# Own-result waits taken out of the mixing stages of a two-block transformer kernel

## The chip, the core and the metric

The kernel runs on one core of one Trainium2 chip. The metric is the device time of one execution in microseconds. Three executions of the kernel before took 4094.2, 4097.06 and 4097.98 us, so the median is 4097.06 us.

## What is computed

The input is 512 tokens of 1024 values. The reference runs two layers of a first block (which is computed in `block1`) and then two layers of a second one (`block2`), all in float32. Cut to what matters here:

```python
# block 1, one layer
h = h + 0.5 * _swiglu_ffn(_rms_norm(h, ffn1_norm[i]), ffn1_w_gate_up[i], ffn1_w_down[i])
u = _rms_norm(h, mix_norm[i])
q, k, v, ca, cg = jnp.split(u @ w_in[i], SPLITS, axis=-1)
attn = _sliding_window_attention(q, k, v, sinks[i])       # 8 heads, window 128, after partial rope
conv = _conformer_conv(ca, cg, ...)                       # 31 taps, layer norm, silu
mixed = jnp.concatenate([_rms_norm(attn, ...), _rms_norm(conv, ...)], axis=-1)
h = h + mixed @ w_out[i]
h = h + 0.5 * _swiglu_ffn(_rms_norm(h, ffn2_norm[i]), ...)
h = h + jax.nn.sigmoid(h @ w_ple_gate[i]) * _rms_norm(p[i] @ w_ple[i], ple_norm[i])
...
# block 2, one layer: the same frame, with three mixers side by side
#   gated delta rule (6 heads, short convolutions, chunks, a running state),
#   sparse attention with a compressed branch (6 heads),
#   stick-breaking attention (4 heads)
# then an FFN with a convolution of 3 taps and the gated per-layer embedding
return _rms_norm(h, final_norm)
```

## The kernel before, in words

Activations lie transposed in SBUF: 128 partitions times 8 chunks of 512 tokens. A weight matrix is streamed from HBM in units of 128 x 1024 values. TensorE (PE) multiplies in a format that drops the low bits of float32, so every weight unit and every activation tile is split in two: ScalarE (ACT) writes the high part (`act_split`, L381), VectorE (DVE) the rest (`dve_split`, L385), and `pe_unit` (L399 to L401) does three matmuls for each chunk. The result of a unit lies in one of two PSUM banks, and VectorE takes it out ("evicts" it).

There is no scheduler. Every engine runs a list of instructions written out by hand, and the engines meet on semaphores: an instruction ends with `.then_inc(s["name"], 1)`, and `wait_ge(s["name"], n)` stands ahead of whichever needs it. In the feed-forward stages ScalarE and VectorE wait for results of their own only where the next operation reads or overwrites them. In the other stages (the "mixing stages") nearly every operation of these two engines is followed at once by a wait for its own semaphore, whatever comes next; `st.up(name)` counts up how far that semaphore is.

The mixing stages of a layer of block 1 are the input projection (14 units), the attention with its convolution, normalisations and per-layer embedding, and the output projection (8 units). The attention runs over 16 pairs of heads and blocks: PE `scores` (L821), VectorE `scale` (L1203, which adds the mask and takes the maximum), ScalarE `exps` (L1003), PE `turn` (L833), VectorE `turn_back` (L1215), PE `values`. Between them stand taps of the convolution on all four engines (L854 PE, L1144 VectorE, L935 ScalarE, L734 GpSimd), the layer norm (L1285 to L1300), and the per-layer embedding, one tile for each pair: PE L807, VectorE L1189, ScalarE L987. At the end come the tiles of the attention output (L1242, PE L860) and their parts (L1312, L1249).

In block 2 the input projection (22 units, evicted by `evict`, L2823 and L2829, with `post` for the rotated tiles, L2791 to L2798) is interleaved with the sparse attention (L2080, L2240, L2149, L2250); then follows the delta rule with its triangular inverse (PE L1748, L1756, L1764; VectorE L1786; ScalarE L1773, L1779) beside the stick-breaking attention (PE L1903, VectorE L1960, ScalarE L1931, L1936), then the running state, the normalised heads (`dve_lo`, `dve_gate`, `act_hi`: L2332, L2308, L2316, L2320; PE L2292), and the embedding (PE L2349, VectorE L2911). After the last layer, VectorE scales the eight chunks of `h` (L2958), and each is stored as it is done.

ScalarE evaluates functions from tables. Where the next function needs another table, an ACT_TABLE_LOAD stands ahead of the ACTIVATE that needs it. An instruction carries one wait; where there are more, the rest are put on what stands ahead of it, the table load or a wait alone in the engine's queue.

## Time and profile before

| | |
|---|---|
| median of three executions | 4097.06 us |
| the profiled execution | 4096.91 us |
| its span, from the first to the last instruction | 4095.1 us |
| granted TensorE clock, mean over the span | 0.965 |
| instructions of VectorE, ScalarE and GpSimd with busy time | 3149, 2242 and 366 |
| VectorE and ScalarE busy | 57% and 39% of the span |

The page of the profile divides the span into busy time by engine. A stage is read by asking for the same sums in a stretch of the span. A timeline lists the instructions of a stretch in order of time; two of one engine whose start and length are both known show whether the second began before the first had ended. The clock is a share of 2.4 GHz: 1.00 is that level, 0.50 is 1.2 GHz.

### The profile page before, as it was taken

To read this page: it belongs to the slowest core of one execution; us is meant where nothing else is said; L and a number is where in the kernel's file an instruction comes from. 1 tells how busy PE (TensorE), PEld (TensorE's weight loads), DVE (VectorE), ACT (ScalarE), POOL (GpSimd) and SP (SyncE) were. 2 spreads that over 40 slices of the span, in tenths; PEclk is the share of its full clock that TensorE was granted. 3 is DMA by queue.
4 is the path that set the end of the run, shared out by engine and by line. 5 is a ranking of instruction groups with operands and counts; after the bars stand their busy time and mean duration, and the time that the engine had idled before them with its cause. 6 is when DMAs were issued, how large, how long until landed. Compare 5 with 4: busy or idle time off the path is not lost. (4 is left out here: it accounts for less than half of the span.)

```text
span 4095.1 us, 47766 instructions
## 1 busy us (share of the span) xinstructions
PE 3912.0 (96%) x17866; PEld 3105.5 (76%) x17866; DVE 2340.5 (57%) x3149; ACT 1583.4 (39%) x2242; POOL 491.2 (12%) x366
## 2 busy tenths in 40 slices
PE   8999989999999997999989989899999999989997
PEld 6888658888788865888867667788877667778886
DVE  5455756445544575645567643675576763376656
ACT  3224643223322464322343534343343444433333
POOL 1001711000000172000020012200010002210002
PEclk9999979999999997999999989899999998999999
DMA  4333103333333320333331100122333100022222
GB/s 148 96 98 110 55 16 98 98 97 108 88 98 97 110 66 13 95 98 98 105 103 62 42 6 1 47 93 98 98 105 100 55 31 1 6 71 94 98 98 77
DMA packets 87028, 315.08 MB, mean 77 GB/s; under 512 B 10016, under 2 KB 10400, under 8 KB 86176
## 3 DMA queue, kind: packets, MB, share of 16 engines
q1 hardware_dynamic: 83664, 302.43, 23.7%
q10 hardware_dynamic: 3152, 9.74, 0.7%
q8 instruction: 143, 2.34, 0.2%
q14 instruction: 69, 0.57, 0.0%
HBM read 307.94 MB, written 2.10 MB: 76 GB/s over the span
## 5 line engine op out<-in xcount | busy, mean ns | idle before, releaser
L381 ACT ACTIVATE wh<-raw 128x1024 fp32r<-128x1024 f32 x564 | 597.8, 1060 | 1613.0 <-PE ps L401 1305.5
L399 PE MATMUL ps<-xh,wh 128*128 128x512 f32 x2336 | 918.3, 393 | 16.8 <-DVE xl L464 10.0
L400 PE MATMUL ps<-xl,wh 128*128 128x512 f32 x2336 | 911.3, 390 | 0.0
L401 PE MATMUL ps<-xh,wl 128*128 128x512 f32 x2336 | 911.1, 390 | 0.0
L385 DVE TENSOR_TENSOR wl<-raw,wh 128x1024 fp32r<-128x1024 f32 x564 | 693.8, 1230 | 201.8 <-ACT wh L381 197.8
L399 PEld LDWEIGHTS ps<-xh,wh 128*128 128x128 f32 x2336 | 440.1, 188 | 113.0 <-issue 20.0
L400 PEld LDWEIGHTS ps<-xl,wh 128*128 128x128 f32 x2336 | 440.1, 188 | 94.3 <-issue 3.6
L401 PEld LDWEIGHTS ps<-xh,wl 128*128 128x128 f32 x2336 | 440.0, 188 | 91.9
L399 PE MATMUL ps<-fh,wh 128*128 128x512 f32 x1016 | 397.3, 391 | 4.4 <-DVE wl L385 4.4
L400 PE MATMUL ps<-fl,wh 128*128 128x512 f32 x1016 | 395.4, 389 | 0.0
L401 PE MATMUL ps<-fh,wl 128*128 128x512 f32 x1016 | 395.3, 389 | 0.0
L443 POOL TENSOR_TENSOR rstd<-rstd,sq 128x512 f32<-128x512 f32 x77 | 116.4, 1512 | 1693.7 <-ACT sq L438 1692.7
L555 DVE SCALAR_TENSOR_TENSOR h<-ps,h 128x512 f32<-128x512 f32 x144 | 99.5, 691 | 317.5 <-PE ps L401 245.4
L399 PEld LDWEIGHTS ps<-fh,wh 128*128 128x128 f32 x1016 | 190.7, 188 | 48.2 <-DVE wl L385 8.3
L401 PEld LDWEIGHTS ps<-fh,wl 128*128 128x128 f32 x1016 | 190.7, 188 | 39.8
L400 PEld LDWEIGHTS ps<-fl,wh 128*128 128x128 f32 x1016 | 190.7, 188 | 39.6 <-issue 0.5
L409 PE MATMUL ps<-xh,wh 128*128 128x512 f32 x448 | 196.6, 439 | 18.6 <-PEq L1363 9.8
L625 DVE TENSOR_TENSOR ubuf<-ps,rstd 128x512 f32<-128x512 f32 x88 | 60.9, 692 | 264.7 <-PE ps L401 264.7
L734 POOL TENSOR_TENSOR y<-y,tap_out 128x512 f32<-128x512 f32 x120 | 173.7, 1448 | 76.7 <-ACT tap_out L935 69.2
L411 PE MATMUL ps<-xh,wl 128*128 128x512 f32 x448 | 178.2, 398 | 0.0
L410 PE MATMUL ps<-xl,wh 128*128 128x512 f32 x448 | 177.7, 397 | 0.0
L621 DVE TENSOR_TENSOR gbuf<-ps,rstd 128x512 f32<-128x512 f32 x88 | 60.9, 692 | 197.8 <-PE ps L401 197.7
(463 smaller groups left out, 5694.7 us busy)
## 6 DMA issues: line engine op xcount, KB each, us to landing
raw<-in_w SPq DMA_DIRECT2D x564, 512.0 KB, 3.5
con<-in_consts SPq DMA_DIRECT2D x1, 2052.5 KB, 14.1
h<-in_x SPq DMA_DIRECT2D x4, 512.0 KB, 7.2
p_t<-in_p ACTq DMA_DIRECT2D x4, 512.0 KB, 3.7
w1k<-in_w1c ACTq DMA_DIRECT2D x2, 1024.0 KB, 4.8
w1v<-in_w1c ACTq DMA_DIRECT2D x2, 1024.0 KB, 7.2
out<-h SPq DMA_DIRECT2D x8, 256.0 KB, 2.1
dup_k<-roped ACTq DMA_DIRECT2D x8, 128.0 KB, 2.8
```

What stands on the lines that cost most here:

```text
L381: nc.scalar.activation(wh[k % 2][:, :], raw[k % 4][:, :], ACT.Copy).then_inc(s["w_hi"], 1)
L385: nc.vector.tensor_tensor(wl[k % 2][:, :], raw[k % 4][:, :], wh[k % 2][:, :].bitcast(F32), ALU.subtract).then_inc(s["w_lo"], 1)
L399: nc.tensor.matmul(DB[k % 2][:, :], a, hi(q), start=(q == order[0]), stop=False)
L400: nc.tensor.matmul(DB[k % 2][:, :], a, lo(q), start=False, stop=False)
L401: last = nc.tensor.matmul(DB[k % 2][:, :], b, hi(q), start=False, stop=(q == order[-1]))
L409: nc.tensor.matmul(DB[k % 2][:, :], a, hi(q), start=start and n == 0, stop=False)
L410: nc.tensor.matmul(DB[k % 2][:, :], a, lo(q), start=False, stop=False)
L411: last = nc.tensor.matmul(DB[k % 2][:, :], b, hi(q), start=False, stop=stop and n == len(chunks) - 1)
L443: nc.gpsimd.tensor_tensor(acc[:, :], acc[:, :], sq[:, n % 2, :], ALU.add).then_inc(s["sq_add"], 1)
L555: nc.vector.scalar_tensor_tensor(h[:, j, :], DB[k % 2][:, :], factor, h[:, j, :], ALU.mult, ALU.add).then_inc(s["bank"], 1)
L621: v.tensor_tensor(gbuf[:, :], DB[k % 2][:, :], rstd[:, :], ALU.mult).then_inc(s["bank"], 1)
L734: nc.gpsimd.tensor_tensor(y[:, ct, :], y[:, ct, :], tap_out[:, i % 3, :], ALU.add)\
```

## The change

On VectorE, ScalarE and GpSimd, the wait for an operation's own semaphore is taken out after nearly every operation of the mixing stages. It stays where the very next operation reads or overwrites the result, and a wait is put in front of later operations that do so (the diff takes out 137 lines with a wait and puts in 25). Increments, instructions and buffers stay as they are. In the built program 1062 instructions of VectorE, 846 of ScalarE and 100 of GpSimd have lost a wait, and 86 of VectorE and 72 of ScalarE name one that they did not name before, partly because a wait has moved from one instruction to its neighbour.

The core of the diff; the same edit is made in some hundred places:

```diff
@@ scale and exps of the attention, block 1
                                     v.tensor_tensor_reduce(sm[:, m % 2, e, 0:w], ...)\
                                         .then_inc(s["max_ready"], 1)
-                                    dve.wait_ge(s["max_ready"], st.up("max_ready"))
...
                                       bias=negm[:, n:n + 1], accum_out=den[:, n:n + 1]).then_inc(s["prob"], 1)
-                                    act.wait_ge(s["prob"], st.up("prob"))
@@ layer norm
                                     for q in range(CT):
                                         v.tensor_tensor(y[:, q, :], y[:, q, :], rstd[:, :], ALU.mult)\
                                             .then_inc(s["ln_ready"], 1)
-                                        dve.wait_ge(s["ln_ready"], st.up("ln_ready"))
@@ a wait that is kept, further down
                             def sink_in(b):
+                                dve.wait_ge(s["max_ready"], (b + 1) * H1)
                                 v.tensor_tensor(es[:, b, 0, :], negm[:, b * H1:(b + 1) * H1], g("sinks"), ALU.add)\
                                     .then_inc(s["sink_in"], 1)
-                                dve.wait_ge(s["sink_in"], st.up("sink_in"))
@@ rotate, block 1
+                                dve.wait_ge(s["bank"], o + U1_IN + (9 if n == 0 else n + 10))
                                 v.tensor_tensor(fbuf[:, :], buf[:, :], cos[:, :], ALU.mult).then_inc(s["dve_step"], 1)
+                                dve.wait_ge(s["rot_mm"], n + 1)
                                 dve.wait_ge(s["dve_step"], st.up("dve_step"))
-                                dve.wait_ge(s["rot_mm"], n + 1)
@@ output projection
                                 v.tensor_tensor(h[:, n, :], DB[u % 2][:, :], h[:, n, :], ALU.add)\
                                     .then_inc(s["bank"], 1)
-                                dve.wait_ge(s["bank"], st.up("bank"))
                                 if n < DC - 1:
                                     dve_split(dve, s, st, 0, u + 2)
+                                dve.wait_ge(s["bank"], u + 1)
                                 dve_tile(dve, s, st, n, g("ffn2"), made + 8 + n)
@@ evict, block 2
                                 if kind in ("rope", "tok"):
-                                    dst = (gbuf, ubuf)[posted.index(n) % 2][:, :]
+                                    p_ = posted.index(n)
+                                    dst = (gbuf, ubuf)[p_ % 2][:, :]
+                                    if due(p_ - 1):
+                                        dve.wait_ge(s["post_done"], p_ - 1)
...
                                     v.tensor_tensor(dst, src, rstd[:, :], ALU.mult).then_inc(s["bank"], 1)
-                                    dve.wait_ge(s["bank"], st.up("bank"))
@@ the last scaling
                                     v.scalar_tensor_tensor(h[:, j, :], h[:, j, :], gfin[:, 8 + j:9 + j], rstd[:, :],
                                                            ALU.mult, ALU.mult).then_inc(s["fin_h"], 1)
-                                    dve.wait_ge(s["fin_h"], st.up("fin_h"))
```

No instruction changes its place on any engine. What changes is what each waits for. On VectorE, in the attention of block 1 (pair 9, then the reciprocal of the layer norm), before and then after; `ISA sm` is `scale`, `ISA negm` the read of its maximum, and line numbers differ between the two texts:

```order
L1203 ISA sm,negm<-ps,con,negsink 128x256 [waits prob,s_mm,pt_ready]
L1203 ISA negm 128x1
L1203 ISA sm,negm<-ps,con,negsink 128x256 [waits max_ready]
L1203 ISA negm 128x1
L1189 COPY e_t<-ps 128x512 [waits ple_mm,max_ready]
L1215 COPY pt<-ps 128x512 [waits pv_mm,pt_mm,ple_ev]
L1221 TENSOR_TENSOR es<-negm,small_73 128x8 [waits pt_ready]
L1290 RECIPROCAL rstd<-rstd 128x512 [waits ln_root,sink_in]
L1293 TENSOR_TENSOR y<-y,rstd 128x512 [waits dve_step]
```

```order
L1181 ISA sm,negm<-ps,con,negsink 128x256 [waits prob,s_mm]
L1181 ISA negm 128x1
L1181 ISA sm,negm<-ps,con,negsink 128x256
L1181 ISA negm 128x1
L1168 COPY e_t<-ps 128x512 [waits ple_mm]
L1192 COPY pt<-ps 128x512 [waits pv_mm,pt_mm]
L1198 TENSOR_TENSOR es<-negm,small_73 128x8 [waits max_ready]
L1260 RECIPROCAL rstd<-rstd 128x512 [waits ln_root]
L1263 TENSOR_TENSOR y<-y,rstd 128x512 [waits dve_step]
```

Every row but the last has lost the wait for the row ahead of it; the last reads what the reciprocal writes and keeps it. On ScalarE, at the root of the layer norm's variance (L1025), before and then after:

```order
L992 ACTIVATE gbuf,ss<-o_tok 128x512 [waits o_ready,prob]
L1025 ACT_TABLE_LOAD [waits var_mm]
L1025 ACTIVATE rstd<-ps,con 128x512 [waits o_sum]
L987 ACTIVATE tap_out<-e_t 128x512 [waits ple_ev,ln_root]
L1003 ACT_TABLE_LOAD [waits max_ready,pt_mm]
```

```order
L981 ACTIVATE gbuf,ss<-o_tok 128x512 [waits o_ready]
L1011 ACT_TABLE_LOAD
L1011 ACTIVATE rstd<-ps,con 128x512 [waits var_mm]
L977 ACTIVATE tap_out<-e_t 128x512 [waits ple_ev]
L991 ACT_TABLE_LOAD [waits max_ready]
```

The ACTIVATE had two waits, and the one for PE's result (`var_mm`) stood on the table load; now it stands on the ACTIVATE, and the load waits for nothing.

## Rows read from the trace of the kernel before

**Rows 1.** The page: TensorE's busy time over the span, its share, instructions.

```profile
PE 3912.0 (96%) x17866; PEld 3105.5 (76%) x17866; DVE 2340.5 (57%) x3149; ACT 1583.4 (39%) x2242; POOL 491.2 (12%) x366
```

**Rows 2.** Busy time by stretch: length, then engines, granted clock, DMA, GB/s.

```profile
716.80:819.20 102.40, 102.40 (x453) 84.79 (x452) 41.91 (x49) 25.44 (x29) 0.00 (x0) 1.00 0.33 98
463.00:606.00 143.00, 116.91 (x424) 75.57 (x424) 81.95 (x156) 70.74 (x139) 56.01 (x44) 0.81 0.04 12
2106.00:2361.00 255.00, 249.98 (x1191) 180.08 (x1189) 185.04 (x339) 109.89 (x180) 9.95 (x7) 0.99 0.20 65
2361.00:2403.00 42.00, 35.54 (x146) 24.48 (x145) 23.39 (x37) 7.84 (x13) 5.34 (x5) 0.67 0.03 13
2403.00:2579.00 176.00, 167.18 (x1134) 138.80 (x1132) 65.14 (x118) 80.10 (x120) 41.40 (x38) 0.97 0.01 4
2579.00:2635.00 56.00, 45.68 (x191) 35.04 (x191) 32.78 (x50) 18.60 (x28) 9.03 (x7) 0.79 0.08 25
2375.40:2406.10 30.70, 27.15 (x85) 17.78 (x86) 11.12 (x22) 7.92 (x11) 5.74 (x6) 0.50 0.00 1
```

**Rows 3.** Waits of TensorE over the span: total us, times, longest.

```profile
PE ps L807 <- DVE e_t L1189: 18.7, 10, 4.9
PE ps L2349 <- DVE e_t L2911: 12.7, 4, 4.7
PE ps L860 <- DVE o_tok L1242: 12.5, 2, 6.2
```

**Rows 4.** Timeline of VectorE, feed-forward stage: start, length, instruction.

```profile
709.47 0.69 DVE L625 TENSOR_TENSOR ubuf<-ps,rstd 128x512 f32<-128x512 f32 x1 [3.06 <-PE ps L401]
710.20 0.69 DVE L628 TENSOR_TENSOR fbuf<-ubuf,sbuf 128x512 f32<-128x512 f32 x1
710.81 1.22 DVE L385 TENSOR_TENSOR wl<-raw,wh 128x1024 fp32r<-128x1024 f32 x1
```

**Rows 5.** Timeline of ScalarE, feed-forward stage, then attention.

```profile
704.09 1.06 ACT L381 ACTIVATE wh<-raw 128x1024 fp32r<-128x1024 f32 x1 [3.41 <-PE ps L401]
705.06 0.61 ACT L613 ACTIVATE sbuf<-gbuf 128x512 f32<-128x512 f32 x1
...
472.81 2.98 ACT L935 ACTIVATE tap_out<-upad,small 128x512 f32<-128x512 f32 x4
476.37 0.72 ACT L935 ACTIVATE tap_out<-upad,small 128x512 f32<-128x512 f32 x1 [0.58 <-POOL y L734]
```

**Rows 6.** Timeline, attention of block 1, layer 0, VectorE and then TensorE.

```profile
540.11 3.35 DVE L1290 RECIPROCAL rstd<-rstd 128x512 f32<-128x512 f32 x1
...
543.50 2.87 DVE L1293 TENSOR_TENSOR y<-y,rstd 128x512 f32<-128x512 f32 x4
546.40 0.48 DVE L1203 CUSTOM_DVE_ANT_0 sm<-ps,con,negsink 128x256 f32<-128x256 f32 x1
...
546.93 0.48 DVE L1203 CUSTOM_DVE_ANT_0 sm<-ps,con,negsink 128x256 f32<-128x256 f32 x1
...
547.46 0.69 DVE L1189 COPY e_t<-ps 128x512 f32<-128x512 f32 x1
...
548.30 0.77 PE L807 MATMUL ps<-p_hi,wh 128*128 128x512 f32 x1 [4.94 <-DVE e_t L1189]
```

**Rows 7.** Timeline of block 2's last mixing stage, layer 1.

```profile
3600.86 0.75 DVE L2308 SCALAR_TENSOR_TENSOR dec<-ps,small,z_t 128x512 f32<-128x512 f32 x1
...
3605.40 0.80 PE L2349 MATMUL ps<-p_hi,wh 128*128 128x512 f32 x1 [4.66 <-DVE e_t L2911]
```

**Rows 8.** Timeline, the last scaling.

```profile
4085.52 6.26 DVE L2958 SCALAR_TENSOR_TENSOR h<-h,gfin,rstd 128x512 f32<-128x512 f32 x8
```

**Rows 9.** Timeline of ScalarE, a table load in the attention.

```profile
531.64 1.28 ACT L1025 ACT_TABLE_LOAD   x1 [4.11 <-PE ps L889]
...
532.94 0.69 ACT L1025 ACTIVATE rstd<-ps,con 128x512 f32<-128x512 f32 x1
```

**Rows 10.** Timeline of VectorE beside GpSimd, end of the input projection.

```profile
463.75 1.48 DVE L1126 TENSOR_TENSOR fbuf<-ubuf,cos 128x512 f32<-128x512 f32 x1
```

More of the change, by code:

```diff
@@ L556, in dve_ffn @@
                                                    ALU.mult, ALU.add).then_inc(s["bank"], 1)
-                    evicted = st.up("bank")
                     if j < DC - 1:
@@ L560, in dve_ffn @@
                     if g == len(GROUPS) - 1 and gain is not None:
-                        dve.wait_ge(s["bank"], evicted)
+                        dve.wait_ge(s["bank"], k + 1)
                         dve_tile(dve, s, st, j, gain, x_n + j, hi, lo)
@@ L621, in dve_swiglu @@
             v.tensor_tensor(gbuf[:, :], DB[k % 2][:, :], rstd[:, :], ALU.mult).then_inc(s["bank"], 1)
-            st.up("bank")
             dve_split(dve, s, st, i, k + 2)
@@ L1158, in _ @@
                                     out = (v_t, ubuf)[n % 2]
+                                    if due(n // 2) and n % 2:
+                                        dve.wait_ge(s["conv_in"], n // 2)
                                 elif n == 9:
@@ L1460, in read @@
                             .then_inc(s["bank"], 1)
-                        st.up("bank")
                     def later_taps(half):
@@ L1579, in dve_rows @@
                         .then_inc(s["dve_step"], 1)
[L1580 removed]
+                    st.up("dve_step")
                     v.memset(ones, 1.0).then_inc(s["dve_step"], 1)
@@ L2790, in post @@
                                 if kind == "rope":
+                                    dve.wait_ge(s["bank"], o + posted[p_] + 1)
+                                    if due(p_):
+                                        dve.wait_ge(s["post_done"], p_)
                                     v.tensor_tensor(sbuf[:, :], buf[:, :], cos[:, :], ALU.mult)\
                                         .then_inc(s["dve_step"], 1)
+                                    dve.wait_ge(s["post_mm"], p_ + 1)
                                     dve.wait_ge(s["dve_step"], st.up("dve_step"))
-                                    dve.wait_ge(s["post_mm"], p_ + 1)
                                     v.tensor_tensor(buf[:, :], BK[p_ % 2][:, :], sin[:, :], ALU.mult)\
@@ L2799, in post @@
                                         .then_inc(s["post_done"], 1)
-                                    dve.wait_ge(s["post_done"], st.up("post_done"))
                                 else:
@@ L2805, in post @@
                                         .then_inc(s["post_done"], 1)
-                                    dve.wait_ge(s["post_done"], st.up("post_done"))
                             def evict(n):
@@ L2919, in _ @@
                                     .then_inc(s["bank"], 1)
-                                dve.wait_ge(s["bank"], st.up("bank"))
                                 if n < DC - 1:
@@ L2926, in _ @@
                                     dve.wait_ge(s["dve_step"], st.up("dve_step"))
+                                dve.wait_ge(s["bank"], u + 1)
                                 dve_tile(dve, s, st, n, g("ffn"), made + n)
@@ L2940, in _ @@
                                     .then_inc(s["bank"], 1)
-                                dve.wait_ge(s["bank"], st.up("bank"))
                                 if n < DC - 2 or n == DC - 2 and after:
```

154 lines of the change are left out of this document (29 added, 125 removed).

## The prediction, made before the changed kernel was run

> **What bounds the kernel now.** I read the page first. TensorE is busy for 3912.0 of 4095.1 us [rows 1]. So 183.1 us of the span are open to a change that does nothing to the matmuls, and the first question is where they lie. The sums by stretch answer it. In a stretch of the feed-forward stage TensorE has no idle time at all, 102.40 of 102.40 us, at full clock. In the attention of block 1 it idles 143.00 - 116.91 = 26.1 us; in block 2's input projection with the sparse attention 255.00 - 249.98 = 5.0 us; in the start of the delta rule 42.00 - 35.54 = 6.5 us; in its main part 176.00 - 167.18 = 8.8 us; and from the running state to the output projection 56.00 - 45.68 = 10.3 us [rows 2]. That is 56.7 us for one layer of each block, some 113 us for both. The rest lies at the start, at the joints of the blocks and after the last matmul. The diff touches nearly only these mixing stages, so this is the place to look.
>
> The second question is who ends TensorE's idle time. The waits say: mostly VectorE. L807 waits 18.7 us for the copy L1189, L860 waits 12.5 us for L1242, and L2349 waits 12.7 us for L2911 [rows 3]. The timeline in front of the longest wait of L807 shows VectorE with no pause: a reciprocal, four multiplications, two `scale`, the copy, each right behind the other, and then TensorE starts after 4.94 us of idleness [rows 6]. That is the kind of place where time between two VectorE instructions becomes time of the kernel.
>
> **What one wait costs.** The feed-forward stage has both kinds of neighbours. L628 reads what L625 writes and waits for it: the starts lie 710.20 - 709.47 = 0.73 us apart, which is L625's 0.69 and 0.03 to 0.04 of gap. L385 behind it has no wait for L628, and starts 710.81 - 710.20 = 0.61 us after it, 0.08 before it has ended [rows 4]. So a wait for an own result costs VectorE 0.73 - 0.61 = 0.12 us when the next instruction is otherwise ready. ScalarE: behind L381 (1.06 us) the Silu without such a wait starts after 705.06 - 704.09 = 0.97 us, 0.09 early. In the attention four L935, which wait each for the one ahead, take 2.98 us; with 0.72 for one, the starts lie (2.98 - 0.72) / 3 = 0.75 apart, 0.03 late [rows 5]. Again 0.12 us. I take 0.12 for both engines.
>
> The Trainium skill speaks against this. "VectorE: DVE Perf Modes", section "The DRAIN you can't avoid", says that eight copies take the same time with a semaphore after each as with one at the end, and its rules advise to count operations and not semaphores; by that the sum below would be 0. The same section sends the reader on to two instructions with no wait between them, where the later one starts early unless it is held, and with that the 0.08 us of [rows 4] agrees. The page's comparison counts increments and not waits, so I give the first reading a chance but not the first place.
>
> **The parts of the change.** Waits go at 1062 instructions of VectorE and 846 of ScalarE. All of them at 0.12 us would be 229 us, more than there is idle time, so the number of waits says nothing; only those in a row of work that TensorE waits for count. I went through the timeline of each mixing stage and counted, in the stretches that end with an idle TensorE, the instructions that start 0.03 to 0.04 us behind their neighbour because of a wait that goes.
>
> - *Attention of block 1.* Ahead of the first scores: 3. Ahead of the long wait of L807: 9 (the four L1293 and two L1203 of [rows 6] with the copies around them). In the next two pairs, through ScalarE's Silu tiles too: 8. At 573 to 575 us: 2. From the reciprocal L1297 to L860: 6. From there to the output projection some 10 stand in a row, but TensorE idles only 0.6 us there, so I count 5. Together 33, times 0.12 is 4.0 us a layer, 8.0 us for two.
> - *Running state to output projection, block 2.* About 10 in the rows that end at L2349 and L2292, as L2308 and its neighbours [rows 7]: 1.2 us, 2.4 for two layers.
> - *Main part of the delta rule.* About 9, mostly the pairs of L1786 and the three L1960: 1.1 us, 2.2 for two layers.
> - *Block 2's input projection and the start of the delta rule.* TensorE idles 11.5 us in them; waits for row operations and norms, where I find few neighbours: 8, so 1.0 us, 2.0 for two layers.
> - *The last scaling.* Eight in a row take 6.26 us and nothing covers them [rows 8]. Seven waits go: 7 x 0.12 = 0.8 us. This is the surest term.
> - *Input and output projections of block 1, the embedding gate.* TensorE is busy there, VectorE waits for it. The work of `pe_unit` hides the edits, and I count 0. They would be worth something only if VectorE were late for a bank.
> - *Table loads.* A load takes 1.28 us. At L1025 it starts after ScalarE has idled 4.11 us for TensorE, and the root follows at 532.94 [rows 9]. In the new program the load waits for nothing and lies inside those 4.11 us, so the root starts 1.28 us earlier. The same is so at a dozen loads, but few of them lead to TensorE. I take 1 us for each layer's attention and 0.3 for the compressed scores of each layer of block 2: 2.6 us.
> - *Waits that are added* (`post_done` at evictions, `bank` at `rotate`, `z_ready` at the squares). Each is for an instruction that stands several places earlier on the same engine. Nothing queues behind them that would not have queued before. From 0 to 0.12 us each, and nearly none on the path; I take 0.
> - *GpSimd's 100 waits.* It is busy 56.01 us in the attention and its sums are ready before they are asked for: 0.
>
> The sum is 8.0 + 2.4 + 2.2 + 2.0 + 0.8 + 2.6 = 18.0 us. The profiled execution took 4096.91 us, 0.15 less than the median, and 4096.91 - 18.0 = 4078.9. I predict **4079 us**.
>
> The bounds. Below, if the waits cost nothing where they stand, it is 0. Above, I count every own wait in the long rows of VectorE that touch an idle TensorE at all, also where TensorE is idle only for a part of them: 75 in an attention stage, about 20 in each of three stages of block 2. That is 2 x (75 + 60) = 270, with the 7 at the end 277, times 0.12 = 33 us, and with the loads 36 us: 4061 us. I stay near the lower of the two counts, since in the other the same idle time is used twice. Also, a pair of the attention goes TensorE, VectorE, ScalarE, TensorE; when one leg is shorter the next is often not ready.
>
> **Rivals.**
>
> *Nothing.* The waits of one engine for another take over: VectorE reaches its next instruction 0.12 us earlier and waits there for TensorE. For it: in the attention VectorE is busy for only 81.95 of 143.00 us, so for much of it it waits for someone. Against it: in front of L807 and L860 it does not. The time would be that of before less the last scaling and the surest loads, 4092 to 4097 us.
>
> *The clock gives back more.* TensorE runs at 0.50 of its clock for all of 2375.4 to 2406.1 us, with 27.15 us of work in it [rows 2]; at full clock that work would take 13.6 us. What went before it is a stretch in which TensorE paused for VectorE. If shorter pauses keep it from falling there in both layers, 2 x 13 = 26 us come on top of a part of the sum: 4055 to 4068 us. For it: the change makes exactly these pauses shorter. Against: they get shorter by a tenth, and the clock falls in the same places in both layers although these differ by some us.
>
> *Slower, by the clock.* The same mechanism the other way. The mixing stages have 0.81, 0.67 and 0.79 of the clock [rows 2]. If TensorE's work comes in tighter bursts between the same long waits, the low level could last longer. At half clock a us of matmuls costs half a us. To undo 18 us and lose 8 more, the low level would have to last 52 us longer, where now a layer's attention has 143 x (1 - 0.81) x 2 = 54 us of it. It decides from 36 us of more low level on, below which the change still gains; the time would be near 4105 us. Nothing in the trace points that way, but one stretch of 30.7 us moved or doubled is a large part of it.
>
> *Slower, by the shared memory.* L1126 takes 1.48 us while GpSimd works beside it [rows 10], and a like operation 0.69 [rows 6]. If VectorE's instructions shift so that more of them meet GpSimd's, each costs 0.8 us. GpSimd's own work stays the same, so what VectorE meets stays about the same in sum; ten more meetings on the path would be needed to take away 8 us. I put it with the rival above.
>
> **How the numbers follow.** A measurement of this kernel cannot tell less than 0.2%, 8.2 us, from no change. My forecast, 8 to 28 us faster: 0.58. More, through the clock: 0.14. Nothing: 0.19. Slower than by 8.2 us: 0.09. That makes faster 0.72, same 0.19, slower 0.09. The range reaches from the clock rival's middle to the middle of the rival in which nothing comes of it: 4057 to 4093 us, which leaves out about 0.05 below and 0.15 above.
>
> **What would show it.** In the profile after, four L1293 should take 2.87 - 3 x 0.12 = 2.5 us and eight L2958 6.26 - 0.8 = 5.4 us; if not, the price is wrong. The longest wait of L807 should fall from 4.9 to about 4, and that of L860 from 6.2 to about 5.5; if these stay while the rows on VectorE are shorter, another wait has taken their place. TensorE's idle time in an attention stage should be near 22 us. The feed-forward stretches should stay as they are. The table load of L1025 should lie before the end of TensorE's L889. The forecast is wrong if the mean clock over the span moves from 0.965 by more than 0.003, which is 12 us of the low level's difference, or if the rows are shorter and TensorE's idle time is not.

## The result, and the profile after

The changed kernel took 4056.95 us (median of four executions, 4049.91 to 4058.68), beside 4095.63 us (4088.59 to 4097.98) for the kernel before on the same chip: a ratio of 0.9904, with a 95% interval of 0.9892 to 0.9917. That is 38.7 us, where 18 were forecast. The direction and the places were right, the size was off by a factor of two, and the time lies just below the range. The profiled execution took 4058.68 us, with a span of 4056.9, against 4096.91 and 4095.1 before.

The page after answers to [rows 1]:

```profile
PE 3895.8 (96%) x17866; PEld 3094.0 (76%) x17866; DVE 2287.4 (56%) x3149; ACT 1543.7 (38%) x2242; POOL 491.6 (12%) x366
```

Here is already a part of the answer. The span has fallen by 38.2 us. TensorE's idle time is 4056.9 - 3895.8 = 161.1, before it was 183.1, so it has fallen by 22.0. The other 16.2 us are TensorE's *busy* time: the same 17866 matmuls took less time. My sum was one of idle time only. (These are two single executions, and the division isn't one by cause, as the executions at equal clock show further down.)

Sums by stretch of the kernel after (length, then PE, PEld, DVE, ACT and POOL busy with their instructions, granted clock, DMA share, GB/s): the attentions of layers 0 and 1 of block 1, block 2's first input projection, the half-clock stretch at the start of its delta rule, and a stretch of the feed-forward stage:

```profile
462.70:595.30 132.60, 110.12 (x425) 71.18 (x424) 75.59 (x157) 65.52 (x139) 55.94 (x44) 0.86 0.04 12
1487.80:1619.30 131.50, 110.36 (x426) 70.73 (x425) 75.04 (x157) 65.66 (x139) 56.09 (x44) 0.86 0.04 13
2062.30:2335.10 272.80, 260.83 (x1232) 188.53 (x1233) 185.07 (x346) 116.60 (x191) 14.99 (x11) 0.98 0.20 66
2348.50:2379.20 30.70, 28.14 (x88) 18.48 (x88) 10.36 (x22) 9.23 (x13) 5.73 (x6) 0.50 0.00 1
703.80:806.20 102.40, 102.40 (x453) 84.81 (x452) 42.40 (x48) 26.45 (x30) 0.00 (x0) 1.00 0.32 96
```

Beside [rows 2]: the feed-forward stretch is untouched, the 30.7 us at half clock are still there in full, and layer 0's attention has gone from 143.0 to 132.6 us at a clock of 0.86 instead of 0.81. Two of the same sums of the kernel before that were not shown, layer 1's attention and the first input projection:

```profile
1500.40:1640.40 140.00, 113.65 (x424) 74.13 (x424) 81.30 (x156) 70.75 (x139) 56.03 (x44) 0.83 0.04 12
2083.80:2362.10 278.30, 264.18 (x1237) 190.51 (x1237) 195.49 (x346) 120.06 (x191) 15.33 (x11) 0.97 0.20 65
```

TensorE's waits over the span after, which answer to [rows 3] (total us, times, longest; L802 was L807, L855 was L860, L2268 was L2349):

```profile
PE ps L802 <- DVE e_t L1168: 13.1, 11, 3.8
PE ps L855 <- DVE o_tok L1217: 12.3, 2, 6.2
PE ps L2268 <- DVE e_t L2818: 11.9, 4, 4.3
```

And the timeline of the kernel after where [rows 6, 8, 9] stood before (start, length, instruction, idle time before it and what ended it):

```profile
524.72 1.28 ACT L1011 ACT_TABLE_LOAD   x1
525.81 0.59 PE L884 MATMUL ps<-ubuf,con 128*128 128x512 f32 x1
526.24 1.02 PE L884 MATMUL ps<-fbuf,con 128*128 128x512 f32 x2
527.30 0.69 ACT L1011 ACTIVATE rstd<-ps,con 128x512 f32<-128x512 f32 x1 [1.29 <-PE ps L884]
...
534.76 3.35 DVE L1260 RECIPROCAL rstd<-rstd 128x512 f32<-128x512 f32 x1
...
538.14 2.50 DVE L1263 TENSOR_TENSOR y<-y,rstd 128x512 f32<-128x512 f32 x4
540.56 0.48 DVE L1181 CUSTOM_DVE_ANT_0 sm<-ps,con,negsink 128x256 f32<-128x256 f32 x1
...
540.96 0.48 DVE L1181 CUSTOM_DVE_ANT_0 sm<-ps,con,negsink 128x256 f32<-128x256 f32 x1
...
541.37 0.69 DVE L1168 COPY e_t<-ps 128x512 f32<-128x512 f32 x1
...
542.20 0.76 PE L802 MATMUL ps<-p_hi,wh 128*128 128x512 f32 x1 [3.80 <-DVE e_t L1168]
...
4047.99 5.39 DVE L2862 SCALAR_TENSOR_TENSOR h<-h,gfin,rstd 128x512 f32<-128x512 f32 x8
```

The price on VectorE was right nearly to the digit: four multiplications take 2.50 us (2.87 before, 2.5 forecast), eight scalings 5.39 (6.26 before, 5.4 forecast), and from the first of these multiplications to TensorE's start it is 4.06 us instead of 4.80. On ScalarE three of the convolution's L929 (L935 before) now stand in a row of 1.93 us, so their starts lie (1.93 - 0.72) / 2 = 0.60 us apart, where it was 0.75. The table load has moved as forecast, ahead of the end of L884.

To see all of it I cut every trace at the same VectorE instructions. Length, in brackets TensorE's idle time, and behind it the time at a granted clock of 0.50, all in us of one execution:

| stage | before | after | expected gain | length's gain | of it idle time |
|---|---|---|---|---|---|
| attention, layer 0 | 143.1 (26.1) 54.6 | 132.6 (22.5) 37.5 | 5.0 | 10.5 | 3.6 |
| attention, layer 1 | 140.0 (26.3) 47.8 | 131.5 (21.1) 37.5 | 5.0 | 8.5 | 5.2 |
| block 2, first projection and start of delta rule | 317.5 (20.4) 43.0 | 310.6 (16.5) 34.5 | 1.3 | 6.9 | 3.9 |
| the same, layer 1 | 307.4 (14.6) 36.7 | 303.3 (11.9) 32.6 | 1.3 | 4.1 | 2.7 |
| main part, both layers | 358.7 (18.8) 22.7 | 357.5 (14.0) 35.2 | 2.2 | 1.2 | 4.8 |
| running state to output, both | 107.9 (22.8) 41.0 | 104.6 (23.0) 34.2 | 2.4 | 3.3 | -0.2 |
| tail | 22.0 (19.9) 19.9 | 21.1 (19.0) 18.8 | 0.8 | 0.9 | 0.9 |
| the rest (feed-forward, block 1's projections, joints, start) | 2698.5 (34.2) 17.0 | 2695.7 (33.1) 13.7 | 0 | 2.8 | 1.1 |

### The profile page after: what moved, and what is told of

It is laid out like the page before. It is cut to its first block and busy times, and to the rows that moved or that the text cites. A ratio compares the mean times of both kernels' runs of the same rounds, so it can differ in the third digit from the quotient of the medians.

```text
span 4056.9 us, 46747 instructions
## 1 busy us (share of the span) xinstructions
PE 3895.8 (96%) x17866; PEld 3094.0 (76%) x17866; DVE 2287.4 (56%) x3149; ACT 1543.7 (38%) x2242; POOL 491.6 (12%) x366
## 3 DMA queue, kind: packets, MB, share of 16 engines
q1 hardware_dynamic: 83664, 302.43, 23.8%
## 5 line engine op out<-in xcount | busy, mean ns | idle before, releaser
L385 DVE TENSOR_TENSOR wl<-raw,wh 128x1024 fp32r<-128x1024 f32 x564 | 694.4, 1231 | 191.7 <-ACT wh L381 190.7
L399 PEld LDWEIGHTS ps<-xh,wh 128*128 128x128 f32 x2336 | 440.0, 188 | 112.6 <-issue 19.9
```

The costliest lines, as they stand in the source:

```text
L385: nc.vector.tensor_tensor(wl[k % 2][:, :], raw[k % 4][:, :], wh[k % 2][:, :].bitcast(F32), ALU.subtract).then_inc(s["w_lo"], 1)
L399: nc.tensor.matmul(DB[k % 2][:, :], a, hi(q), start=(q == order[0]), stop=False)
```

## The experiments

Each was timed beside the kernel before on the same chip. A ratio is to that one. Times of both kernels scatter by up to 12 us between executions, so I read a stage from the trace, and the sum from the ratio. A trace is one execution, and its clock scatters too.

**Executions at equal clock.** Every execution lists its mean granted clock, and the time goes with it. Of 75 executions of the kernel before, timed beside the experiments, the 16 at 0.965 took 4098.95 us on average, and the six at 0.970 took 4089.29 us (4088.69 to 4089.70). The changed kernel's five at 0.970 took 4057.65 us (4055.61 to 4058.68). At the same mean clock the change is worth 31.6 us, then, and only some 7 of the 38.7 us come with the higher clock, although TensorE's busy time differs by 16.2 us in the two traces. (An equal mean doesn't say that the clock is low in the same places.)

**One engine at a time.** The same diff, its lines for VectorE alone (`e1_vector_only`), and for ScalarE alone (`e2_scalar_only`):

```diff
-                                    dve.wait_ge(s["max_ready"], st.up("max_ready"))     # e1, and so on
...
-                                    act.wait_ge(s["prob"], st.up("prob"))               # e2, and so on
```

> Only VectorE's part of the change; ScalarE and GpSimd wait for their own results as before. Own waits theory (most of the gain lies in VectorE's rows ahead of TensorE's waits, L807 and L860 above all): 25 to 32 us faster than before, TensorE idle some 15 us less and busy some 12 us less. Rival, ScalarE's early table loads and its own waits carry half or more: under 18 us faster.

> Only ScalarE's part of the change, early table loads with it; VectorE and GpSimd as before. Own waits of VectorE as the main cause: 4 to 10 us faster. Rival, ScalarE carries half or more: 18 us faster or more. If the parts add up, this and the kernel with VectorE's part alone give 38 us together; if the two engines stand in one another's way, each alone gives less than its share.

VectorE alone: 4072.11 us (4068.34 to 4072.65), 0.9944 [0.9928, 0.9961], or 21.4 us. ScalarE alone: 4089.91 us (ten executions, 4083.41 to 4097.5), 0.9990 [0.998, 1.0], or 3.6 us, less than can be told from no change. Both are below what I had expected, 25 to 32 and 4 to 10 us. VectorE carries most of it, but together they make 25 us of 38.7. In the traces TensorE's idle time falls by 17.5 and 4.1 us, together 21.6 of the 22.0: idle time adds up. What doesn't is the rest, TensorE's busy time. In the attention stages the kernel with VectorE's part has the idle time of the changed one (21.8 and 21.9 us, against 22.5 and 21.1), but 44.4 us of half clock in each instead of 37.5, and takes 134.6 and 134.8 us. GpSimd's 100 waits are in neither kernel, and no run takes them out alone. That they are worth nothing is not shown; the idle times leave 0.4 us for them.

**The early table loads undone.** In the changed kernel, a wait for something long past is put ahead of ScalarE operations that follow a load. With it the wait that matters stands on the load again (of 102 loads 60 had a wait before, 32 after, 56 here):

```diff
+                                    act.wait_ge(s["stat_read"], 1)
                                     act.wait_ge(s["var_mm"], 1)
```

> The changed kernel with one long-satisfied wait in front of some 24 of ScalarE's operations that need another table, so that the wait for the other engine stands on the table load again, as before the change. The prediction's term (2.6 us for early loads): 2 to 5 us slower than the changed kernel. Rival, the early loads carry the excess over the forecast: 10 to 20 us slower than the changed kernel, so 18 to 28 us faster than before.

It took 4057.38 us, 0.9908 [0.9891, 0.9924], which can't be told from the changed kernel's 0.9904. Its attentions take 132.5 and 131.5 us, as in the changed kernel, and block 2's input projections 274.3 and 266.7 us instead of 272.8 and 266.4. The load of the layer norm's root starts behind TensorE again, timeline of ScalarE in this kernel:

```profile
526.87 1.28 ACT L1012 ACT_TABLE_LOAD   x1 [2.63 <-PE ps L884]
528.17 0.69 ACT L1012 ACTIVATE rstd<-ps,con 128x512 f32<-128x512 f32 x1
```

The root is late by nearly a us and nobody minds: its reader, the reciprocal L1260, starts only at 534.76 us in the rows above, when VectorE has come to it. Of my 2.6 us for the loads the 2 for the attentions were 0. For the other 0.6 the trace leaves room in the first projection, where half clock differs too (13.7 and 10.2 us); it isn't resolved.

**TensorE kept busy.** If busy time has fallen because the clock was low for less time, then matmuls that nobody needs, put into TensorE's pauses, should do a part of the same to the kernel before. The first version repeats matmuls that are there (`rotate(4)` four times more, `values` of pairs 10, 11 and 15 three, one and four times, the last embedding tile once):

```diff
-                                for e in range(2):
+                                for e in (0, 1) * FILL_VALUES.get(m, 1):      # {10: 4, 11: 2, 15: 5}
```

> The kernel before with all its waits; TensorE repeats matmuls that it does anyway, with the same inputs into the same bank, in five places of each attention stage of block 1 just ahead of its long idle times (four more of the last rotation, 3 and 1 more passes of the values of pairs 10 and 11, one more of the last embedding tile, 4 more of the values of pair 15). VectorE's and ScalarE's work is unchanged. Clock theory (shorter idle times keep TensorE's clock up, and that gave the other half of the gain): 8 to 16 us faster than before, with less time at clock 0.50 in 463 to 606 us. Rival, the clock's lower share in the low level was only a by-product: no change or up to 6 us slower.

4090.38 us (ten executions, 4088.8 to 4092.95), 0.9991 [0.9982, 1.0001]. Half clock fell to 30.7 and 27.3 us in the two attentions, and they got shorter by 3.3 and 1.7 us although TensorE has more to do. The kernel as a whole is 3.1 us faster than the 4093.48 us beside it, which can't be told from no change; I had expected 8 to 16.

The second puts more of them in, 9 ahead of the first scores, 12 ahead of L860 and some in three embedding tiles, in the kernel before and in the changed one:

```diff
+                            def filler(times):
+                                for _ in range(times):
+                                    mm(BK[4][:, :], c("ident"), cos[:, :], start=True, stop=True)
...
+                            filler(9)
                             scores(0)
```

> The kernel before with all its waits; TensorE fills its five long idle times in each attention stage of block 1 with 128x512 matmuls whose results nothing reads (9 ahead of the first scores, 12 ahead of L860) and with repeats of the embedding tiles 3, 4 and 7 (3, 1 and 2 more passes). The fills before were short matmuls of 64 columns and left a stretch of 20.5 us at clock 0.50. Clock theory: this stretch goes or shrinks too, the low level takes under 20 us of an attention stage (now some 50), each stage is 5 to 9 us shorter and the kernel 8 to 16 us faster than before. Rival, the low level costs nothing where TensorE waits anyway: low level shorter, time as before within 3 us.

> The changed kernel with the same fills. Clock theory: 5 to 12 us faster than the changed kernel, 42 to 50 us faster than before. Rival (the change has taken already what the clock can give): the same as the changed kernel within 3 us, or slower by the fills.

Before with it: 4094.13 us (4089.3 to 4097.29), 0.9997 [0.9988, 1.0006]. After with it: 4064.29 us (4056.98 to 4065.46), 0.9921 [0.9908, 0.9935]. Neither came near what the clock theory had asked for, 8 to 16 us and 42 to 50; the changed kernel without the fill took 4058.14 us in the same batch. From the one kernel with the fill to the other it is 29.8 us, at a median clock of 0.977 in both. Layer 1's attention is the clean pair, first the kernel before with the fill, then the changed one with it:

```profile
1499.20:1636.80 137.60, 126.23 (x503) 78.56 (x503) 81.99 (x158) 70.80 (x139) 56.13 (x44) 0.99 0.04 12
```

```profile
1485.30:1616.90 131.60, 126.01 (x503) 78.50 (x502) 75.76 (x156) 65.40 (x139) 55.99 (x44) 0.99 0.04 13
```

At a clock of 0.99 in both, TensorE's busy time is the same and the stage differs by 6.0 us (5.8 where it is cut at the same instructions): this is what the waits alone are worth where the clock plays no part. My count of 33 and 0.12 said 4.0. (Layer 0's pair, 142.9 and 131.6 us, isn't clean: its clocks are 0.93 and 0.99.) And without a wait taken out, the clock and the fill make 140.0 into 137.6. The changed kernel gains nothing by the fill (131.6 against 131.5), although it has 34 us less of half clock. The fill puts 15.7 us more of matmuls into the stage, so what it costs and what the clock gives back can't be told apart here. That low clock costs little where TensorE waits for the others anyway fits this, and isn't shown by it.

**Waits that I hadn't counted, put back.** In the changed kernel, 33 of VectorE's own waits for an attention stage return at pairs 0 to 8, at two embedding tiles and in the layer norm:

```diff
                                         .then_inc(s["max_ready"], 1)
+                                    if m <= 8:
+                                        dve.wait_ge(s["max_ready"], 2 * m + e + 1)
```

> The changed kernel with VectorE's own waits put back at 33 places of each attention stage that I had not counted, since TensorE is not idle behind them: the maxima and copies of pairs 0 to 8, two embedding tiles and the subtraction of the mean. The prediction's count: at most 2 us slower than the changed kernel. Rival, VectorE's row is what bounds the stage and every wait in it counts: 33 x 0.12 x 2 = 8 us slower.

> The changed kernel once more, beside the others on one chip: 35 to 40 us faster than before.

4062.66 us (4061.76 to 4066.98), 0.9924 [0.991, 0.9937], beside the changed kernel again in the same batch: 4058.14 us (4051.39 to 4061.90), 0.9909 [0.9895, 0.9923]. That is 4.5 us, between the 2 at most of my count and the rival's 8, with intervals that overlap. In the traces the stages are longer by 3.0 and 3.6 us (134.7 and 135.2 against 131.7 and 131.6). In layer 0 the waits themselves make up only 0.6 us of it: that is how much later VectorE has come, from the start of the stage, by 548 us. TensorE's idle time is 21.8 and 20.9 us against 21.2 and 21.1. The rest shows itself in two timelines of TensorE over the same pairs, first this kernel, then the changed one:

```profile
545.37 2.07 PE L816 MATMUL ps<-k_t,q_t 64*128 64x256 f32 x4
...
554.37 2.07 PE L816 MATMUL ps<-k_t,q_t 64*128 64x256 f32 x4
...
564.69 1.13 PE L816 MATMUL ps<-k_t,q_t 64*128 64x256 f32 x4
```

```profile
545.64 2.07 PE L816 MATMUL ps<-k_t,q_t 64*128 64x256 f32 x4
...
554.65 1.31 PE L816 MATMUL ps<-k_t,q_t 64*128 64x256 f32 x4
...
562.59 1.13 PE L816 MATMUL ps<-k_t,q_t 64*128 64x256 f32 x4
```

Up to 554 us the two run side by side. Then four scores take 2.07 us in the one and 1.31 in the other, and the next ones come 10.32 instead of 7.94 us later. The clock rows say why: the half-clock stretch begins at 540.2 and lasts 20.5 us here, and 13.7 us, from 541.4, there:

```profile
540.20:560.70 20.50, 16.73 (x49) 12.46 (x50) 9.50 (x24) 12.10 (x25) 8.81 (x7) 0.50 0.09 27
```

```profile
541.40:555.10 13.70, 10.86 (x29) 7.80 (x30) 6.48 (x16) 10.17 (x19) 7.51 (x6) 0.50 0.14 40
```

So 6.8 us more of half clock cost 2.4 us at this place. Was it the waits that set it off, or chance? The same stretch is 20.5 us long in layer 1 of this kernel too. In five traces with all of block 1's change and no fill it is, over both layers, 13.7 us seven times and 17.0 three times (once in two pieces), and never 20.5. So it was the waits; which of them is not known.

**One block at a time.** The diff's lines up to the end of `block1` only (with a few helpers that both blocks share), and those of `block2` only.

> The change in the code of block 1 (and the few lines shared by both), block 2 as before. My theory now: the attention stages give some 11 and 8.5 us as in the whole change, block 2 nothing, so about 20 us, 4075 us on a before of 4095; half clock in the two attention stages near 37.5 us each. By the first forecast (5.0 us for a stage) it would be 10 to 11 us. If the blocks help each other (a stage of block 2 that gains only because block 1 ended otherwise) it would be more or less than 20 by over 3 us.

> Block 2 changed, block 1 as before: the counterpart of the run with block 1 alone, which gave 23.8 us. If the blocks add, this one gives the rest, 38.3 less 23.8 or some 15 us: 4080 us on 4095.5, with the stages of block 2 as long as in the whole change (272.9, 37.8, 179.5, 52.4 and 266.4, 37.0, 178.0, 52.4) and the attentions at 143.1 and 140.0. If the gain of a block needs the other, it is off by over 3 us.

Block 1 alone: 4071.39 us (4069.86 to 4073.56), 0.9941 [0.9928, 0.9954], 23.8 us. Block 2 alone: 4080.63 us (4077.99 to 4084.76), 0.9965 [0.9951, 0.9978], 14.3 us. Sum 38.1, where the whole gave 38.7: within the noise the blocks add. The expectation was 3.8 us short for block 1 and held for block 2. For both the prediction was too low: 10 and 8 us. With block 1 the median clock rises from 0.966 to 0.971, with block 2 it stays at 0.966. In the trace of block 2 alone its stages, from its first projection on and with the tail, are 14.0 us shorter, 11.5 of them idle time, and half clock takes 162.7 us in them instead of 163.3. So block 2's gain came without a higher clock: here it was the waits that I had put too low.

**The clock held at full level.** 41 fillers for a stage, better placed and without repeats of real work: ahead of the first scores, ahead of two embedding tiles into the bank of the statistics, ahead of the last `turn` and of L860:

```diff
+                                if m == 11:
+                                    pe.wait_ge(s["ln_root"], 1)
+                                if m in (11, 12):
+                                    filler({11: 10, 12: 4}[m], STAT)
                                 if PLE_AT <= m < PLE_AT + DC:
```

> The kernel before with 41 matmuls of 128x512 more in each attention stage, of the identity and into banks that nobody reads then, put where TensorE idles longest (ahead of the first scores, ahead of two embedding tiles in mid stage, ahead of the last turn, ahead of L860). No wait of the change is gone. Clock theory: half clock falls from 54.6 and 47.8 us a stage to under 20, the stages shorten by 3 to 4 and by 2 to 3 us, to about 139.5 and 137.5, all of it 5 to 7 us of the kernel. If the whole gain of the change comes from waits alone, nothing: both stages stay at 143 and 140 although the clock is up.

> The same 41 matmuls a stage in the changed kernel. Clock theory: it has already got what the clock gives on the path, so the stages stay at 131.5 to 132.5 us and the time within 3 us of the changed kernel, 4057. Against the kernel with the same matmuls and the old waits the stages differ by the waits alone: 5.8 us as in the pair of dense kernels, 7 at most. If low clock still costs in the changed kernel, it gains 3 us or more and is the best version.

Before: 4090.69 us, 0.9986 [0.9978, 0.9995]. After: 4064.03 us, 0.9927 [0.9914, 0.994]. One of the first kernel's twelve executions took 5807.67 us, at a mean granted clock of 0.632; why the clock was low is not known, and the median doesn't depend on it. From the one to the other it is 26.7 us, at a median clock of 0.980 and 0.979. Layer 0's attention, before and then after, both with the fill:

```profile
461.60:601.40 139.80, 133.41 (x507) 78.28 (x507) 81.93 (x157) 70.72 (x139) 56.05 (x44) 1.00 0.04 12
```

```profile
461.00:596.40 135.40, 133.26 (x507) 78.23 (x506) 75.87 (x157) 65.36 (x139) 56.11 (x44) 1.00 0.04 12
```

At full clock the waits are worth 4.4 us here, and 6.1 in layer 1 (141.4 and 135.3). The clock theory was only half right: of the kernel before layer 0's stage is shorter by 3.3 us, but layer 1's is 1.4 longer than in the trace shown above. The changed kernel loses 2.8 to 3.8 us a stage by the fill, and there TensorE idles for only 2.1 us: what I put into pauses may have become the bound. No version with a fill beats the changed kernel; this one was expected within 3 us of 4057.

**The input projection of block 2.** The prediction had 1.0 us a layer for its waits and those of the delta rule's start behind it, and 0.3 for loads; "nothing", as the first expectation below has it, was my count for block 1's projections. First the waits are put back into the changed kernel, for VectorE (and at one place for ScalarE):

```diff
                                     v.tensor_tensor(dst, src, rstd[:, :], ALU.mult).then_inc(s["bank"], 1)
+                                    dve.wait_ge(s["bank"], st.up("bank"))
```

> The changed kernel, with VectorE's own waits put back in block 2's input projection alone (the row operations on 6 partitions, evictions, post-processing of rotated tiles, convolution outputs, the scaling of block 1's last result). My theory: at its start the projection is bound by VectorE, which has no pause from 2114 to 2132 us, so these waits, some 10 to 15 per layer in rows that TensorE waits behind, carried what I had priced at nothing. The projection of layer 0 gets longer by 3 to 5 us (272.9 to about 277), that of layer 1 by 1 to 2 (266.4 to about 268), and the kernel to some 4062. Rival (my forecast: TensorE is busy there, VectorE waits for it, the edits are hidden): both stay within 0.5 us and the 5.5 us of layer 0 came from how block 1 ended or from ScalarE; the kernel stays at 4057.

Its five executions fall on two values, 4051.85 to 4052.79 and 4062.84 and 4064.65 us; the median of 4052.79, 0.9900 [0.9886, 0.9913], says nothing for the expected 4062. The two values differ in clock, 0.972 and 0.969. The changed kernel's executions took 4049.91 and 4051.39 us at 0.972, and 4059.39 and 4061.90 at 0.969, so at equal clock the waits cost 1.5 and 3.1 us by these few executions. In the trace (which is of a long execution) the projections take 276.7 and 267.1 us instead of 272.8 and 266.4, the first with 2.2 us more of idle time and 3.5 more of half clock. So the opposite was tried, these waits alone taken out of the kernel before:

> The kernel before, with VectorE's own waits taken out in block 2's input projection alone: the opposite of the run before, in which the stages got longer by 3.8 and 0.7 us in the trace while the times fell on two values 11 us apart and told nothing. If these waits carry the gain of the projection, layer 0's gets shorter by 3.5 to 5 us from 278.3 and layer 1's by 0.5 to 1.5 from 268.2, and the median by 4 to 6 us, to 4090 or 4091 on a before of 4095.5. If the edit is hidden and the 5.5 us come from ScalarE or from block 1, both stay within 0.5 us.

4090.73 us (eleven executions, 4087.61 to 4101.19), 0.9987 [0.9978, 0.9996], or 4.2 us. In its trace the first projection is shorter by 1.8 us and the start of the delta rule behind it by 1.8; in layer 1 by 0.6 and 0.6. That is 4.8 us by the trace and 4.2 by the times, more than the rival's 0.5 us a stage allows, and in layer 0's projection less than the 3.5 to 5 us that I had expected. But TensorE's idle time in that projection is 14.1 us as before; what fell is half clock, from 17.1 to 13.7 us there and from 25.9 to 22.2 in the delta rule's start. So this run shows that the edit matters, and not that its 0.12 us add up to the gain. (The traced execution as a whole is the longest of the eleven: the main part of layer 0's delta rule takes 185.1 instead of 179.2 us in it, with 22.1 us of half clock instead of 11.6.) Where a wait reaches TensorE is to be seen in VectorE's timeline, before:

```profile
2115.65 3.35 DVE L2864 RECIPROCAL fbuf<-fbuf 128x512 f32<-128x512 f32 x1
2119.03 0.68 DVE L1575 SCALAR_TENSOR_TENSOR cbuf<-cbuf,ybuf 6x512 f32<-6x512 f32 x1
2119.75 0.47 DVE L1578 TENSOR_SCALAR cbuf<-cbuf,tiny 6x512 f32<-6x512 f32 x1
2120.38 0.48 DVE L1581 MEMSET cbuf<- 6x512 f32 x1 [0.16 <-DVE cbuf L1578]
2120.90 1.75 DVE L1584 TENSOR_TENSOR_SCAN rows_t<-cbuf 6x128 f32<-6x128 f32 x4
2122.68 0.68 DVE L1588 TENSOR_TENSOR rows_t<-rows_t 6x512 f32<-6x512 f32 x1
2123.40 0.69 DVE L2823 TENSOR_TENSOR vc_t<-ps,rstd 128x512 f32<-128x512 f32 x1
2124.13 1.22 DVE L385 TENSOR_TENSOR wl<-raw,wh 128x1024 fp32r<-128x1024 f32 x1
```

and after:

```profile
2091.74 3.35 DVE L2771 RECIPROCAL fbuf<-fbuf 128x512 f32<-128x512 f32 x1
...
2096.88 1.36 DVE L1545 TENSOR_TENSOR_SCAN rows_t<-cbuf 6x128 f32<-6x128 f32 x4
2098.28 0.69 DVE L1550 TENSOR_TENSOR rows_t<-rows_t 6x512 f32<-6x512 f32 x1
2098.99 0.69 DVE L2733 TENSOR_TENSOR vc_t<-ps,rstd 128x512 f32<-128x512 f32 x1
2099.60 1.22 DVE L385 TENSOR_TENSOR wl<-raw,wh 128x1024 fp32r<-128x1024 f32 x1
```

VectorE has no pause here, and the split (L385) that TensorE's next unit needs stands at the end of the row. From the reciprocal to it the row takes 7.86 instead of 8.48 us. TensorE's wait for L1588 falls from 1.9 to 0.2 us with the whole change, and to 1.4 with these waits alone, while its two waits for the split L385 take 1.4 and 1.9 us together, after 1.0 before.

The same run shows, by chance, what the clock does to code that nobody touched. Layer 1's attention in this kernel is word for word that of the kernel before:

```profile
1498.40:1641.60 143.20, 116.94 (x425) 75.61 (x425) 81.84 (x156) 70.69 (x139) 56.04 (x44) 0.81 0.04 12
```

TensorE idles for 26.3 us, as in the 140.00 us shown above, and is busy for 116.94 instead of 113.65: 3.3 us more, at 54.6 instead of 47.8 us of half clock. VectorE's and ScalarE's busy times differ by under 0.6 us. With block 2 alone changed this stage was 143.2 us long too.

## Why the prediction was wrong in size, and where it was right

*The bound and the places.* Right. TensorE's pauses behind VectorE in the mixing stages were what the change could reach; block 1 and block 2 gave all of it, the feed-forward stretch nothing.

*The price of 0.12 us.* Right, as the four L1263 and the eight L2862 show, and with it the last scaling (0.8 forecast, 0.9 measured). On ScalarE the three L929 say 0.15. The Trainium skill, "VectorE: DVE Perf Modes", section "The DRAIN you can't avoid", finds eight copies with a semaphore after each as fast as with one after the last. By that the gain would have been nothing, and the runs disagree: what costs here is the wait of the next instruction, and the section doesn't say whether its copies wait.

*The waits on the path, 14.6 us and 0.8 for the tail.* This is the first step that failed. I had two counts of the waits that matter, and took the lower, "since in the other the same idle time is used twice". At equal clock the whole change gives 31.6 us, and with a fill in both kernels 29.8 and 26.7, where the lower count and the loads had 18.0 and the upper 36. In the attention the lower count nearly held (idle time came to 22.5 and 21.1 us, as forecast, and the longest wait of L807 to 3.8): 4.0 us a stage, and with the fill in both kernels 6.0, 4.4 and 6.1 (the upper had 9.0). In block 2 it didn't: with an unchanged clock 14.3 us for my 8.0, where the upper count with its loads would have had 15.8. The projection has a part in it: with the delta rule's start behind it I had 2.6 us for both layers, where the whole change gives 11.0, half clock included. "TensorE is busy there, VectorE waits for it" was my reason for block 1's projections; I had looked at block 2's no better, and at its start VectorE has no pause. Which of its waits carry the gain stays open.

*The table loads, 2.6 us.* Wrong: 0 for the 2 us in the attentions, unresolved for the other 0.6. I saw that the load moved, and didn't look at who reads the root, and when.

*The clock, taken as 0.* This is the second step that failed, and by about as much: 7 us by the executions at equal clock, 9 to 12 by the pairs with a fill. The rival had it at 0.14, and thought of the stretch of 30.7 us, which stayed (27.3 us in layer 1 of the changed kernel). The clock's gain came in small pieces instead. At a granted clock of 0.50 TensorE spends 244.0 us after, 282.7 before, 38.7 less (by chance the figure of the gain), and its busy time is 16.2 us shorter; at twice the speed one would expect up to 19.4. Not all of this was won, though: where TensorE waits for the others, matmuls that end sooner make it wait longer, and at equal clock the kernels still differ by 31.6 us. My bound for it, 0.003 of the mean clock, was passed (0.965 to 0.970), which the prediction named as its falsifier; it was a poor one, since the kernel before alone runs at 0.965 to 0.970 from one execution to the next. The last two waits up to L860 show how the clock enters a wait. Before, then after:

```profile
580.71 1.12 PE L833 MATMUL ps<-con,prob 128*128 128x128 f32 x4 [3.60 <-ACT prob L1003]
...
591.36 1.97 PE L860 MATMUL ps<-con,o_tok 128*128 128x128 f32 x8 [6.23 <-DVE o_tok L1242]
```

```profile
571.96 0.65 PE L828 MATMUL ps<-con,prob 128*128 128x128 f32 x4 [3.42 <-ACT prob L991]
...
581.35 1.97 PE L855 MATMUL ps<-con,o_tok 128*128 128x128 f32 x8 [6.14 <-DVE o_tok L1217]
```

From the one to the other it is 9.39 us instead of 10.65. The wait itself is only 0.09 shorter (I had forecast 0.7), because TensorE, no longer at half clock (0.65 instead of 1.12 us for the same four transposes), comes to it sooner as well. A wait's length is the difference of two arrivals, and both had moved.

*The rivals.* "Nothing" fell. "Slower, by the clock" has a true core: in block 2's main part half clock rose from 22.7 to 35.2 us in the two traces, and of 4.8 us less idle time only 1.2 were left. This isn't the chance of one trace: in seven traces with all of block 2's change it is 26.3 to 41.6 us, in five with none of it 10.6 to 22.7. "Shared memory" is not seen: GpSimd's busy time is the same and VectorE's fell by 53.1 us. The like operation of 0.69 us that this rival compares L1126 with is L628 in [rows 4]; the 0.69 of [rows 6] is a copy.

*The range.* It was said to reach from the middle of the clock rival to that of "nothing". These are 4061.5 and 4094.5 us, not 4057 and 4093, and with the middle as its end it would have missed the time by more.

*What stays open.* The 38.7 us can't be divided exactly. By idle and busy time it is 22.0 and 16.2, by the executions at equal clock 31.6 and 7. But the fills never gave the kernel before more than 3.3 us in an attention stage, where its busy time fell by 3.3 to 6.9 us, and they cost something themselves. That fewer waits cause shorter half-clock stretches is shown at one place of the attention, by the 33 waits put back; for the other places it is inferred from the traces, and in block 2's main part it went the other way.

## What to carry to other kernels

In this kernel a wait for an own result was worth its 0.12 us at most in a row of work without a pause at whose end TensorE stands idle; look for such rows also at the start of stages that look bound by TensorE on average. Where two counts of such rows differ by a factor of two, put both into the range. Add up idle time and busy time separately, and expect that a change in TensorE's pauses changes both: in stages whose clock is below 1.00, put the clock's share into the range (here some 7 to 12 of 38.7 us). It could not be read from the longest half-clock stretch. And before you call a difference of busy time the clock's, compare executions of both kernels that have the same mean clock: the times of single executions are there for it. When an instruction moves earlier, price it at its reader, not at itself.

## What the runs showed of the hardware

- On VectorE an instruction starts 0.12 us later behind one whose result it waits for: four in a row take 2.87 or 2.50 us, eight 6.26 or 5.39.
- A half-clock stretch changes in jumps: with 33 waits put back, which by then had cost 0.6 us, it is 20.5 us long instead of 13.7, and that costs 2.4 us.
- The same code with the same idle time of TensorE takes 140.0 or 143.2 us, with 47.8 or 54.6 us at the low level.
- The time of an execution goes with its mean clock. In the kernel before, 0.965 and 0.970 lie 9.7 us apart, with 41 us of half clock between them; in the changed one 0.969 and 0.972 lie 10.0 us apart (two executions each), with 24 us between them.
- At the start of the delta rule the clock stays at 0.50 for 23.9 to 30.7 us in one piece in all versions, though TensorE is busy for 28.14 of 30.70 us there after the change.
- Fills raise the clock of layer 0's attention from 0.81 to 1.00, and the stage gets at most 3.3 us shorter; what the fill itself costs is in this.
